# Two attentions of a block run as one pipeline of steps, and Silu of the gates is made of an exponential, a reciprocal and a product

## What is computed

```python
# layer a
q, k, v, qm, gate = split(rms_norm(x) @ a_w_in)          # 768, 768, 768, 256, 1024
o  = diff_attention(rope(norm(q)), rope(norm(k)), v)     # 6 heads, causal: softmax map 0 - lam * softmax map 1
o  = rms_norm(o) * (1 - lambda_init)
om = memory_attention(qm, mem)                           # 4 heads of 64, 256 keys, plain softmax
x  = x + (concat([o, om]) * silu(gate)) @ a_w_out
# layer b
q, qm, gate = split(rms_norm(x) @ b_w_in)
o  = stick_breaking_attention(q, k_sb, v_sb)             # 12 heads, causal, built of sigmoids
om = memory_attention(qm, mem)
x  = x + (concat([o, om]) * silu(gate)) @ b_w_out
```

## Time and profile before

| what | value |
|---|---|
| time, median of 3 runs | 2409.64 us (2406.78 to 2412.56) |
| profiled execution | 2410.18 us, span 2408.1 us |
| granted TensorE clock, mean | 0.978 |
| TensorE busy | 2232.8 us, 93% of the span |
| VectorE, ScalarE, GpSimd busy | 1160.6, 948.1, 1132.0 us |
| HBM traffic | 79 GB/s over the span |

### The profile page before, as it was taken

The page is one execution under the profiler, slowest core; times in us unless marked ns, Lnnn a source line. Parts: engine busy times, 40 slices in busy tenths (PEclk is TensorE's granted clock), DMA queues, the critical chain, the costliest instruction groups (busy, mean ns, idle before and its releaser), DMA issues.

```text
span 2408.1 us, 27366 instructions
## 1 busy us (share of the span) xinstructions
PE 2232.8 (93%) x9994; PEld 1697.3 (70%) x9994; DVE 1160.6 (48%) x1815; ACT 948.1 (39%) x1585; POOL 1132.0 (47%) x1364
## 2 busy tenths in 40 slices
PE   6898778998888999999999999889999999999996
PEld 4576446874566766888888788656668888887885
DVE  6786766237745435005318754263340153197542
ACT  3546653235633444223223732334442332237322
POOL 3553125451233422556557585443234575475751
PEclk8999989999999999999999999999999999999998
DMA  3221112221022212233233232212123322232321
GB/s 129 70 88 54 35 62 79 88 88 34 29 70 63 86 53 72 95 105 95 81 96 100 69 112 88 88 50 72 53 71 105 96 91 88 93 104 64 113 88 61
DMA packets 52981, 191.43 MB, mean 79 GB/s; under 512 B 6000, under 2 KB 6256, under 8 KB 52336
## 3 DMA queue, kind: packets, MB, share of 16 engines
q1 hardware_dynamic: 51552, 184.44, 24.5%
q10 hardware_dynamic: 1296, 5.24, 0.6%
HBM read 187.56 MB, written 2.10 MB: 79 GB/s over the span
## 4 chain that ended last, share of the span: by engine, by line
PE 78%; DVE 8%; ACT 7%; issue 3%; POOL 2%; DMA 1%; ACTq 0%; DVEq 0%; SPq 0%
PE proj L500 20%; PE proj L502 20%; PE proj L501 20%; PE score L496 2%; PE turned L496 2%; PE stat L496 2%; POOL lower L452 2%; PE mix L496 2%; PE score L500 2%; PE score L501 2%; PE score L502 2%; PE ptp L710 2%; DVE small L1524 1%; PE proj L496 1%; DMA raw_ring<-stream 1%
## 5 line engine op out<-in xcount | busy, mean ns | idle before, releaser
L452 POOL TENSOR_TENSOR lower<-raw_ring,upper 128x256 fp32r<-128x256 f32 x1360 | 1131.8, 865 | 1232.7 <-ACT upper L1037 1232.7
L500 PE MATMUL proj<-h,upper 128*128 128x512 f32 x1504 | 612.1, 407 | 31.6 <-issue 16.8
L502 PE MATMUL proj<-h,lower 128*128 128x512 f32 x1504 | 590.0, 392 | 0.0
L501 PE MATMUL proj<-h,upper 128*128 128x512 f32 x1504 | 589.2, 392 | 0.0
L1037 ACT ACTIVATE upper<-raw_ring 128x1024 fp32r<-128x1024 f32 x340 | 356.3, 1059 | 549.0 <-PE proj L500 388.8
L500 PEld LDWEIGHTS proj<-h,upper 128*128 128x128 f32 x1504 | 285.0, 190 | 97.2 <-issue 26.2
L502 PEld LDWEIGHTS proj<-h,lower 128*128 128x128 f32 x1504 | 284.2, 189 | 61.5
L501 PEld LDWEIGHTS proj<-h,upper 128*128 128x128 f32 x1504 | 285.2, 190 | 57.7 <-issue 4.3
L500 PE MATMUL proj<-y,upper 128*128 128x512 f32 x664 | 268.8, 405 | 9.8 <-ACT yf L1113 3.5
L501 PE MATMUL proj<-y,upper 128*128 128x512 f32 x664 | 263.8, 397 | 0.0
L502 PE MATMUL proj<-y,lower 128*128 128x512 f32 x664 | 263.7, 397 | 0.0
(11 more groups left out here) (365 smaller groups left out, 3192.3 us busy)
## 6 DMA issues: line engine op xcount, KB each, us to landing
raw_ring<-stream SPq DMA_DIRECT2D x340, 512.0 KB, 3.5
x<-x_in SPq DMA_DIRECT2D x4, 512.0 KB, 7.5
rows<-rows_in ACTq DMA_DIRECT2D x2, 1024.0 KB, 5.2
out<-x SPq DMA_DIRECT2D x8, 256.0 KB, 2.0
memraw<-mem_in SPq DMA_DIRECT2D x1, 1024.0 KB, 11.2
memraw<-mem_in ACTq DMA_DIRECT2D x1, 1024.0 KB, 4.9
rot<-tables_in ACTq DMA_DIRECT2D x2, 512.0 KB, 3.3
ws<-ws_in ACTq DMA_DIRECT2D x2, 256.0 KB, 5.6
```

The source lines that it names most:

```text
L452: ins = nc.gpsimd.tensor_tensor(lower[:, p % RING, a:b], raw_ring[:, p % RAWS, a:b], upper[:, p % RING, a:b].bitcast(FP32), ALU.subtract)
L500: first_ = nc.tensor.matmul(o, lhsT[0], rhs[0], start=start, stop=False)
L501: nc.tensor.matmul(o, lhsT[0], rhs[1], start=False, stop=False)
L502: return first_, nc.tensor.matmul(o, lhsT[1], rhs[0], start=False, stop=stop)
```

## The change

1. `run` takes a list of kinds and walks over the steps of both attentions as one sequence: diff then mem in layer a, stick then mem in layer b. Each kind keeps its own distances ahead and after. So scores, maxima and exponentials of the mem attention start while the last steps of the other one run, and the finish of the last tile falls among the mem steps. A `Bases` object holds the counters' starts of each kind. The waits for the normed q and k of the mem attention and for its values stand ahead of both.
2. Silu of all gates of layer a and of the last two of layer b: ScalarE writes Exp(-z) and a plain copy of z (`exp_gate`), VectorE adds 1 and limits to 1e30, takes the reciprocal and multiplies by z (`by_gate`). VectorE does it at the step after the gate's last unit; for the very last gate, right before the last gated product. ScalarE needs no other table for it in layer a.
3. Gate units: the two mem gates are spread over all 16 steps (one unit per step), the six stick gates end three steps earlier.
4. The first four output jobs run as a `group`: for each tile of y one product triple for each of the four, in four banks. The other four stay as they were. `group` itself existed before.
5. Small ones: the wait of ScalarE for `std_used` ahead of the mem attention moves to the first copy that uses that space; the homes of transposed probabilities are chosen accordingly; a gate's job is read by the copy.

The diff, cut to its core:

```diff
-    def run(kind, ahead, now, after):
-        steps = steps_of(kind)
-        for z in range(-max(d for _, d in ahead), len(steps) + max(d for _, d in after)):
-            for f, d in ahead:
-                if 0 <= z + d < len(steps):
-                    f(z + d, *steps[z + d])
+    def run(kinds, ahead, now, after):
+        steps = [step for kind in kinds for step in steps_of(kind)]
+        for z in range(-max(d for _, d, _ in ahead), len(steps) + max(d for _, d, _ in after)):
+            for f, d, kind in ahead:
+                if 0 <= z + d < len(steps) and steps[z + d][0] == kind:
+                    f(*steps[z + d])
...
-        steps = {"diff": 4 * MT, "stick": 8 * MT, "mem": 8}[kind]
+        steps = {"diff": 4 * MT, "stick": 8 * MT - 3, "mem": 16}[kind]
...
-            if s == "a":
-                attention(S, C, "diff", diff_ops, lambda t, e, kb: v1[:, kb, t * P:t * P + P],
-                          [(lambda t: squares(S, C, c("ones"), 1), 2)], gates)
...
-            attention(S, C, "mem", mem_ops, lambda t, e, kb, l=l: vm[:, l, kb, t * P + HD * e:t * P + HD * e + HD],
-                      gates=gates)
-            added_squares(S, C, s, lambda d: full(S, C, W, f"{s}.out{d}", y, lambda k: ("y", s, k)))
+            if s == "a":
+                attention(S, C, {"diff": (diff_ops, lambda t, e, kb: v1[:, kb, t * P:t * P + P]), "mem": mem_part},
+                          [(lambda kind, t: squares(S, C, c("ones"), 1), 2, "diff")], gates)
...
+            def outs(d):
+
+                if d == 0:
+                    group(S, C, W, names(f"{s}.out", 4), y, lambda k: ("y", s, k))
+                elif d >= 4:
+                    full(S, C, W, f"{s}.out{d}", y, None)
...
-            def silu_gate(t):
-                take(S, C, yf1[:, t, :], ACT.Silu, keys_=[("silu", s, t)], bank_=proj[0], later=True)
+            def exp_gate(kind, t):
+                t = MT + t if kind == "mem" else t
+                j = next_job(S, C, True)
+                act.wait_ge(*S.after("job", j))
+                tables()
+                nc.scalar.activation(yf1[:, t, :], proj[0][:, :], ACT.Exp, scale=-1.0).then_inc(*S.mark("taken", ("exp_gate", s, t)))
+                if t >= MT:
+                    act.wait_ge(*S.after("unit", main_units - 1))
+                nc.scalar.activation(gate_input(t), proj[0][:, :], ACT.Copy).then_inc(*S.mark("taken", ("read", j), ("gate_input", s, t)))
...
-                attention(S, C, "diff", [(mix_square, 1), (lambda t: root(S, C, 1.0 / P), 2)], silu_gate)
-                silu_gate(MT - 1)
+                attention(S, C, ["diff", "mem"], [(mix_square, 1, "diff"), (lambda kind, t: root(S, C, 1.0 / P), 2, "diff")],
+                          exp_gate)
...
-            attention(S, C, "mem", gates=lambda t: silu_gate(MT + t))
+            exp_gate("mem", 1)
...
+                g = yf1[:, t, :]
+                dve.wait_ge(*S.after("exp_gate", s, t))
+                link(S, nc.vector.tensor_scalar(g, g, 1.0, 1.0e30, ALU.add, ALU.min))
+                link(S, nc.vector.reciprocal(g, g))
+                dve.wait_ge(*S.after("gate_input", s, t))
+                link(S, nc.vector.tensor_tensor(g, g, gate_input(t), ALU.mult), ("silu", s, t))
...
+            def mem_finish(t, tile):
+                if t:
+                    by_gate("mem", 1)
+                gated(S, yf1[:, MT + t, :], tile, s, MT + t)
```

More of the change, by code:

```diff
@@ L667, in heads, with attention @@
                     summed()
-        def attention(S, C, kind, score_ops, value, after=(), gates=None):
-            width = P if kind in ("diff", "mla") else HD
+        def attention(S, C, parts, after=(), gates=None):
+            kinds = list(parts)
             scores4, ptps = beside if gates else apart
-            b0, s0, tile0 = C.n["map"], C.n["step"], C.n["tile"]
+            at = Bases(C, kinds)
+            b0 = C.n["map"]
             for j in (1, 2):
@@ L700, in scores, with now @@
                             .then_inc(*S.mark("scored", ("score", b)))
[L702 removed]
+            def now(previous, kind, z, t, e, i):
                 s = C.next("step")
@@ L723, in mixing @@
             def mixing():
-                t, heads_ = late[0][0], [e for _, e, _ in late]
-                tile, s = tile0 + t, late[-1][2]
+                kind, t, heads_ = late[0][0], late[0][1], [e for _, _, e, _ in late]
+                tile, s = at.tile[kind] + t, late[-1][3]
                 late.clear()
+                width = P if kind in ("diff", "mla") else HD
                 pe.wait_ge(*S.after("pt", s))
@@ L1168, in now @@
                     feed_one()
-            ahead = [(breaks, 3)] if kind == "stick" else [(exps, 2)]
             u0 = C.n["unit"]
@@ L1173, in attention @@
                 act.wait_ge(*S.after("unit", u0 - 1))
-            if kind in ("stick", "mem", "mla"):
+            if kinds[0] in ("stick", "mla"):
                 act.wait_ge(*S.after("std_used", C.n["norm"] - 1))
-            run(kind, ahead, now, after)
-            C.n["unit"] += len(tiles_of(kind)) * len(tiles_of(kind)[0])
-            C.n["map"] += maps(kind) * len(steps_of(kind))
+            run(kinds, [(breaks, 3, kind) if kind == "stick" else (exps, 2, kind) for kind in kinds], now,
+                list(after) or [(lambda kind, t: None, 1, kinds[0])])
+            C.n["unit"], C.n["map"] = at.end["unit"], at.end["map"]
         S, C = first, Counts()
@@ L1552, in now @@
-            def now(z, t, e, i):
-                C.next("step")
-                aside(z)
-                if gates and z and gate_done(kind, z - 1) is not None:
-                    gates(gate_done(kind, z - 1))
-            run(kind, ahead, now,
-                [(lambda t: finish(t, C.next("tile")), {"diff": 3, "mla": 2}.get(kind, 1))])
-            C.n["map"] += maps(kind) * len(steps_of(kind))
+            def now(previous, kind, z, t, e, i):
+                C.next("step")
+                aside(kind, z)
+                if gates and previous and gate_done(*previous[0:2]) is not None:
+                    gates(previous[0], gate_done(*previous[0:2]))
@@ new lines, in attention @@
+            ahead = []
+            for kind in kinds:
+                if kind == "stick":
+                    ahead += [(sticks, 2, kind)]
+                else:
+                    ahead += [(maxima, 2 if kind == "diff" else 3, kind), (weights, 1, kind)]
+            run(kinds, ahead, now, [(lambda kind, t: finish[kind](t, at.tile[kind] + t), {"diff": 3, "mla": 2}.get(kind, 1), kind)
+                                    for kind in kinds])
+            C.n["map"], C.n["tile"] = at.end["map"], at.end["tile"]
@@ L1676, in dve_program @@
             else:
-                attention(S, C, "stick", stick_finish, gates=by_gate)
-            def split_main(z, s=s):
-                if z % 2 == 1 and z // 2 < MT:
-                    split(S, y[:, z // 2, :, :], yf1[:, z // 2, :], ("y", s, z // 2))
-            attention(S, C, "mem", lambda t, tile: gated(S, yf1[:, MT + t, :], tile, s, MT + t), split_main, lambda t: None)
+                attention(S, C, {"stick": lambda t, tile: gated(S, yf1[:, t, :], tile, "b", t), "mem": mem_finish},
+                          split_main, by_gate)
@@ L1732, in early @@
                     split_b(z - 19 if z < 27 else 4)
-            attention(S, C, "mla", lambda t, tile: gated_pair(S, t, tile), early, gates=lambda t: None)
+            attention(S, C, {"mla": lambda t, tile: gated_pair(S, t, tile)}, early, gates=lambda kind, t: None)
             for k in range(5, KT):
```

190 lines of the change are left out of this document (104 added, 86 removed).

## The result

| kernel | median us | runs | profiled execution, span |
|---|---|---|---|
| before | 2409.7 (2406.8 to 2412.6) | 4 | 2410.2, 2408.1 |
| changed | 2434.6 (2432.7 to 2437.3) | 4 | 2432.7, 2430.8 |

The ratio is 1.0101, with a 95% interval of 1.0089 to 1.0114: the change makes the kernel 1% slower, 24.9 us, where 2403.5 us were forecast. The miss is 31.1 us, and the time lies 4.6 us above the range of 2398 to 2430.

The account below looks back on a forecast made before the run. VectorE was taken to pace the diff attention, with TensorE partly idle at the seams. First block -6.2 + 3.2 = -3.0 and second -3.8 gave -6.8 from 2409.6, 2402.8, rounded up to 2403.5 us; range 2398 to 2430.

Parts of the forecast that it names:

- R: VectorE's reciprocal of 512 columns in each gate, taken at 0.94 us.
- rival (a): Gates: slow reciprocal, its extra paid by eight gates less 1 us; 2419 us at 3.0, 2437 at 5.3; chance 0.40.
- The formula of the tile: Diff attention: VectorE's work 14.25 + 1.22 + 0.94 = 16.41, with waits and GpSimd 17.5 us per tile against 17.27.
- eight gates on the path: Of ten gates, eight lengthen the path: five diff, two in the first memory part, one in the second.
- Total work the same: Stick attention: gates end three steps earlier, 45 for 48, with total work unchanged and no cost counted.
- A new stall of +3.2: First block's group of outputs: TensorE waits for the fourth weight slot, +3.2 us.
- +1.4: Second block's group of outputs: TensorE waits for the fourth weight slot, +1.4 us.
- VectorE's eight sums: Output jobs: VectorE catches up eight sums, at most 3.4 us each, by the eighth job 22 us later: hidden.
- The first seam: From the last finish inside the diff loop, 293.9, to the first output job: 340.4 instead of 346.59, -6.2 us.
- The second seam: From the last stick product, 640.9, to the second block's output: 679.1 against 684.33, -5.2 us, -3.8 with its stall.
- rival (b): Both seams: mem steps keep their waits, 7 us are lost again, 2410.5 us, no change; chance 0.15.
- signs of being wrong: Reciprocal over 1.7 us, diff tiles near 20, or a seam long as before with TensorE waiting for VectorE's weights.

Follow-up runs that it names:

- experiment 2: Changed kernel with two plain VectorE instructions of 0.43 us each in place of the reciprocal: 2423.1 us, ratio 1.0053.
- 5: Changed kernel with the stick gates spread over 48 steps again instead of 45: 2425.6 us, ratio 1.0062.
- 6: Changed kernel with ScalarE told one gate earlier to split the weights of the fourth output: 2428.0 us, ratio 1.0071.
- 14: Changed kernel with two plain instructions for the reciprocal, stick gates over 48 steps and the fourth output's slot one gate earlier: 2407.5 us, ratio 0.9983.
- experiment 11: Changed kernel with Silu from its own table again, stick gates over 48 steps and the eight outputs one after the other: 2395.1 us, ratio 0.9936.
- experiment 12: Changed kernel with the inverse on ScalarE, VectorE's gate product at tile end, 48 stick-gate steps and the fourth slot one gate earlier: 2403.3 us, ratio 0.9964.
- 8: Changed kernel with the gate's inverse made on ScalarE as exp(-ln(1+e)) instead of VectorE's reciprocal: 2420.7 us, ratio 1.0040.
- 9: Changed kernel with the inverse on ScalarE and VectorE's product of gate and inverse moved to the end of the tile: 2421.0 us, ratio 1.0038.
- 4: Changed kernel with Silu from its own table again, leaving the joined attentions, the output group and the 45 stick-gate steps: 2420.8 us, ratio 1.0037.
- 13: Changed kernel with the inverse on ScalarE, VectorE's gate product at tile end, 48 stick-gate steps and the outputs one after the other: 2398.6 us, ratio 0.9948.
- 10: Changed kernel with Silu from its own table again, stick gates over 48 steps and the fourth output's slot one gate earlier: 2400.2 us, ratio 0.9963.

## Why the prediction was wrong

Of the miss of 31.1 us, 11.5 are the reciprocal (experiment 2), 8.9 the stick gates' steps (5) and 6.6 the slot (6); added they give 27.0, taken away together 2434.6 - 2407.5 = 27.1 (14). The last 4.0 us, 2407.5 for 2403.5, were not isolated by a run. Measured against the kernel before in each one's own session, whose median wandered by 2 us, the three are 13.2, 9.9 and 7.5 us and 2.0 us are left, so the remainder is known to 2 us at best.

- **The step that failed first: R.** I took the reciprocal at 0.94 us "since the second column's step is the nearest row". It takes 3.35 us. I read a slope from two points of which the first doesn't lie on the line, and multiplied it by 510. The other reading of the same rows, 10 ns over its neighbour paid for each column, gave 5.3 us: too much, but the right kind of answer, and it stood in the text as rival (a). By the Trainium skill ("VectorE: DVE Perf Modes", the section on the fixed hardware budget) the repeat count of 8 came to 4.3 us; at that page's 0.96 GHz the measured 6.25 ns a column are six cycles (an estimate), so the measurement doesn't bear out eight, but the rule was far nearer than my slope.
- **What R costs.** The formula of the tile held: 17.5 + (3.35 - 0.94) = 19.9, measured 19.89; at 0.86 it gives 17.4, measured 17.7. I counted eight gates on the path, five in the diff attention, two in the first memory part and one in the second. All six of the diff attention paid, 13.2 us at their end. In the first memory part one of the two is off the path and the other saved 1.3 us for 2.5, since the plain instructions in the reciprocal's place doubled beside GpSimd; the stretch got 0.9 us shorter. In the second memory part it is 43.0 us for 45.8 from the last stick product to the first output. These stretches of two single executions make more than the 11.5 us of the medians, and what gives the rest back was not followed.
- **The stick gates.** "Total work the same" was right (85.3 and 85.5 us of TensorE), and the step was wrong: I moved gate work by three steps and did not ask what then stands between a gate's last product and the next gate's first. It was the mixing, 2.4 us. Nor did I ask what fills TensorE in the three steps that lose their gate units: nothing did, the clock fell, and VectorE waited 5.0 us for the last mixing. A term of nothing measured 5.4 us in waits for the reads, 3.3 at the seam, and 8.9 us in time.
- **The slot.** "A new stall of +3.2" and "+1.4": measured 2.66 and 0.84, and 3.54 with Silu. The mechanism and the size hold. Left out was the low clock behind it, 1.6 us. Undoing the wait gave 6.6, for 4.6 in the sum; the rest was not traced.
- **VectorE's eight sums** were not hidden: TensorE waits 1.4 us for the first of them.
- **The first seam** closed as forecast. In the kernel at the forecast's price (experiment 2) the last finish inside the diff loop starts at 296.3, for 293.9, and from there to the first output product it is 46.7 us, for 46.5; VectorE waits 2.4 us in it, for 1.9. Of the 2.6 us by which its first output product comes late, 2.4 lie in the diff tiles.
- **The second seam** did not. From the last stick product to the first output it is 45.8 us in the changed kernel, 45.0 before, and 38.2 (640.9 to 679.1) were forecast. VectorE waits 7.5 us in it where the sum had 0.7, and TensorE waits 9.2 us for VectorE's weights. That is rival (b)'s picture in one of the two seams, and one of the signs of being wrong that I had named. The steps without gate units are 3.3 us of it and the reciprocal is 2.8. With both undone (experiment 14) it is 41.4 us, VectorE's waits still 3.2; with 48 steps and less gate work on VectorE it is 38.1 (Silu, experiment 11) and 38.5 (experiment 12), at a granted clock of 1.00 for 0.89.
- **Rival (a)** is the case that came, but not alone. By its own rule the measured R gives 2403.5 + 8 x 2.41 - 1 = 2421.8 us, inside the range. R alone cost less than that rule has it, 11.5 us for 18.3. The time left the range by the stick gates, which stood at nothing in the sum, and by what the slot cost beyond its 4.6 us.

## What to carry to other kernels

Don't read an instruction's rate from operands of one or two columns: take a long one, or measure the width, before it goes into an engine that sets the pace. Where a step count or a schedule moves, look at each reuse of a buffer and ask what work now stands between its last reader and the next writer; the same total work can wait 5 us more. Ask too which steps are left without the work that kept an engine busy. Undo the parts of a change one at a time: here the joined attentions are worth 16 us (2411.1 to 2395.1) once Silu stays, the gates keep their 48 steps and the outputs stay apart, while the change as a whole costs 25.

## What the hardware showed that I had not expected

The reciprocal on VectorE costs 153 ns and 6.25 ns a column, 4.8 times a product of two tensors of 512 columns (0.69 us), and its length did not move beside GpSimd: all ten took 3352 to 3354 ns, one of them with GpSimd's subtractions over 1.9 us of it. The add just ahead of it ran from 426 to 973 ns. An exponential and a logarithm more on ScalarE for each gate cost the kernel nothing against Silu with its two table loads while the other costs stood (8 and 9 beside 4), and 3.1 to 3.5 us once they were gone (12 and 13 beside 10 and 11).
